# Dilated attention: row maxima subtracted and rows summed by VectorE, one exponential for three heads on ScalarE

## The reference, cut to what matters

```python
s = jnp.einsum('brhnqd,brhnkd->brhnqk', qb, kw).astype(F32) * (1.0 / math.sqrt(Dh))
s = jnp.where(mask, s, -1e30)
mx = jnp.max(s, axis=-1, keepdims=True)
p = jnp.exp(s - mx)
den = jnp.sum(p, axis=-1, keepdims=True)
o = jnp.einsum('brhnqk,brhnkd->brhnqd', (p / den).astype(v.dtype), vw)
lse = (mx + jnp.log(den))[..., 0]
...
alpha = jax.nn.softmax(jnp.stack(lses, axis=0), axis=0)
o_a = jnp.sum(alpha[..., None] * jnp.stack(outs, axis=0).astype(F32), axis=0).astype(dt)
```

## Time and profile before

| | us |
|---|---|
| median of three runs | 3615.83 |
| lowest, highest | 3612.37, 3620.40 |
| profiled execution | 3621.54 |
| its span, first to last instruction | 3619.9 |

### The profile page before, as it was taken

How to read it: one execution, slowest core, us unless ns; L and a number is a source line. 1 busy time by engine, 2 the same in 40 slices (tenths; PEclk the granted TensorE clock), 3 DMA queues, 4 the chain that set the end, 5 groups by cost and what they waited for, 6 DMA issues and landing times. The chain is left out here.

```text
span 3619.9 us, 45917 instructions
## 1 busy us (share of the span) xinstructions
PE 3258.0 (90%) x17716; PEld 2952.0 (82%) x17716; DVE 1596.1 (44%) x3321; ACT 1164.2 (32%) x2456; POOL 483.8 (13%) x854
## 2 busy tenths in 40 slices
PE   6899988998876999999978899879988779999998
PEld 6789876887766799999878898768877668999997
DVE  5345256453345334434453442564434453344434
ACT  4334423554422221111143334235553222121111
POOL 0111311211233000000001114112112220000000
PEclk9899998999997999999988999999999979999999
DMA  3434433333455122112043344333335551222111
GB/s 128 132 98 132 129 126 98 112 91 99 145 141 162 47 70 70 54 50 70 30 131 96 104 132 126 125 101 105 94 100 156 131 169 35 66 70 70 54 50 64
DMA packets 273050, 358.60 MB, mean 99 GB/s; under 512 B 27128, under 2 KB 209592, under 8 KB 272856
## 3 DMA queue, kind: packets, MB, share of 16 engines
q1 hardware_dynamic: 214520, 182.59, 17.0%
q0 software_dynamic: 58336, 173.45, 15.5%
HBM read 261.27 MB, written 94.69 MB: 98 GB/s over the span
## 5 line engine op out<-in xcount | busy, mean ns | idle before, releaser
L1648 PE MATMUL ps<-wh,xh 128*128 128x384 f32 (+1 forms) x1536 | 579.3, 377 | 19.3 <-DVE wl L1259 6.6
L1649 PE MATMUL ps<-wl,xh 128*128 128x384 f32 (+1 forms) x1536 | 563.8, 367 | 0.0
L1650 PE MATMUL ps<-wh,xl 128*128 128x384 f32 (+1 forms) x1536 | 563.7, 367 | 0.0
L1259 DVE TENSOR_TENSOR wl<-wraw,wh 128x1024 fp32r<-128x1024 f32 (+2 forms) x210 | 232.3, 1111 | 429.0 <-ACT wh L1000 429.0
L1648 PE MATMUL ps<-xh,wh 128*128 128x384 f32 (+1 forms) x1056 | 374.0, 354 | 38.2 <-DVE ol L1345 14.9
L1718 PE MATMUL ps<-xh,wh 128*128 128x384 f32 x1408 | 361.1, 337 | 20.1 <-DVE arena L1635 15.3
L1649 PE MATMUL ps<-xl,wh 128*128 128x384 f32 (+1 forms) x1056 | 360.3, 341 | 0.0
L1650 PE MATMUL ps<-xh,wl 128*128 128x384 f32 (+1 forms) x1056 | 360.2, 341 | 0.0
L1718 PE MATMUL ps<-xl,wh 128*128 128x384 f32 x1408 | 359.0, 336 | 0.0
L1718 PE MATMUL ps<-xh,wl 128*128 128x384 f32 x1408 | 358.8, 335 | 0.0
L1648 PEld LDWEIGHTS ps<-wh,xh 128*128 128x128 f32 x1536 | 299.0, 195 | 55.1 <-DVE ol L1345 7.1
(11 more groups left out here) (211 smaller groups left out, 5315.8 us busy)
## 6 DMA issues: line engine op xcount, KB each, us to landing
wraw<-in_w_in SPq DMA_DIRECT2D x96, 512.0 KB, 4.1
wraw<-in_w_ffn_in SPq DMA_DIRECT2D x88, 512.0 KB, 4.0
wraw<-in_w_in SPq DMA_DIRECT2D x72, 384.0 KB, 3.4
wraw<-in_w_ffn_out SPq DMA_DIRECT2D x44, 512.0 KB, 3.4
qkv_a<-stage POOLq DMA_DIRECT2D x108, 192.0 KB, 2.2
gate_t<-stage POOLq DMA_DIRECT2D x96, 192.0 KB, 2.2
stage<-gate_t POOLq DMA_DIRECT2D x96, 192.0 KB, 2.8
mix_t<-stage POOLq DMA_DIRECT2D x64, 192.0 KB, 3.8
```

Source lines behind the costliest of these rows:

```text
L1259: dve.tensor_tensor(wl[:, half, j, 0:w], wraw[:, n % RAW, 0:w], wh[:, half, j, 0:w].bitcast(F32), ALU.subtract).then_inc(w_lo, 1)
L1648: pe.matmul(out, ah, bh, start=first, stop=False)
L1649: pe.matmul(out, ah, bl, start=False, stop=False)
L1650: return pe.matmul(out, al, bh, start=False, stop=last)
```

## The change

ACT's six exponentials of a unit, with bias and accumulated sum, become two over three heads each, without either. DVE's two small instructions that wrote the negated scaled maxima become two subtractions of the maxima from the masked scores, in place in `a_p`, over three heads each; each raises `a_mx` as its predecessor did. In `a_turn` DVE waits for `a_pr` and sums the rows of all six heads in one instruction, ahead of its wait for the turn and its copy. In `a_out` DVE waits for its own sum ahead of its copy. The step list is the same.

```diff
--- before.py
+++ after.py
@@ -1087,12 +1087,10 @@
                         elif kind == "a_score":
                             u = step[1]
                             nk = len(UNITS[u][3])
-                            for h in range(A_H):
-                                if h % (A_H // 2) == 0:
-                                    act.wait_ge(a_mx, 2 * u + 1 + h // (A_H // 2))
-                                pr = a_p[:, h * nk * P:(h + 1) * nk * P]
-                                ins = act.activation(pr, pr, ACT.Exp, bias=unit_s[:, h:h + 1], scale=HD ** -0.5,
-                                                     accum_out=a_o[:, u % 2, A_W + A_H + h:A_W + A_H + h + 1])
+                            for i in range(2):
+                                act.wait_ge(a_mx, 2 * u + 1 + i)
+                                pr = a_p[:, i * (A_H // 2) * nk * P:(i + 1) * (A_H // 2) * nk * P]
+                                ins = act.activation(pr, pr, ACT.Exp, scale=HD ** -0.5)
                             ins.then_inc(a_pr, 1)
                         elif kind == "a_turn":
                             u = step[1]
@@ -1366,22 +1364,32 @@
                             if u >= 2:
                                 dve.wait_ge(a_stored[u % 2], 16 * A_STORES[u - 2][u % 2])
                             mk = masks[:, mask_of(g, s, t), :]
+
+                            def below(i):
+
+                                hs = slice(i * A_H // 2, (i + 1) * A_H // 2)
+                                part = a_p[:, hs.start * nk * P:hs.stop * nk * P].rearrange("p (h n) -> p h n", n=nk * P)
+                                top = a_o[:, u % 2, A_W + hs.start:A_W + hs.stop]
+                                return dve.tensor_tensor(part, part, top.unsqueeze(2).to_broadcast([P, A_H // 2, nk * P]),
+                                                         ALU.subtract)
+
                             for h in range(A_H):
                                 if h == A_H // 2:
                                     chain.wait()
-                                    dve.tensor_scalar(unit_s[:, 0:h], a_o[:, u % 2, A_W:A_W + h], -HD ** -0.5, None,
-                                                      ALU.mult).then_inc(a_mx, 1)
+                                    below(0).then_inc(a_mx, 1)
                                 sl = slice(h * nk * P, (h + 1) * nk * P)
                                 chain(dve.tensor_tensor_reduce(
                                     a_p[:, sl].rearrange("p (k n) -> p k n", k=nk),
                                     score_bank(nk, h).rearrange("p (k n) -> p k n", k=nk), mk, 1.0, -3e38, ALU.add, ALU.max,
                                     a_o[:, u % 2, A_W + h:A_W + h + 1]))
                             chain.wait()
-                            dve.tensor_scalar(unit_s[:, A_H // 2:A_H], a_o[:, u % 2, A_W + A_H // 2:A_W + A_H],
-                                              -HD ** -0.5, None, ALU.mult).then_inc(a_mx, 1)
+                            below(1).then_inc(a_mx, 1)
                         elif kind == "a_turn":
                             u = step[1]
                             nk = len(UNITS[u][3])
+                            dve.wait_ge(a_pr, u + 1)
+                            chain(dve.tensor_reduce(a_o[:, u % 2, A_W + A_H:], a_p[:, 0:A_H * nk * P].rearrange(
+                                "p (h n) -> p h n", h=A_H), AX_X, ALU.add))
                             dve.wait_ge(a_ptr, u + 1)
                             at = turned(nk)
                             dve.tensor_copy(a_pt[:, 512 * nk:768 * nk], side[:, at + 512 * nk:at + 768 * nk]
@@ -1389,6 +1397,7 @@
                         elif kind == "a_out":
                             u = step[1]
                             dve.wait_ge(a_pv, u + 1)
+                            chain.wait()
                             dve.tensor_copy(a_o[:, u % 2, 0:A_W], side[:, unit_out(u):unit_out(u) + A_W]).then_inc(a_ov, 1)
                         elif kind == "a_merge":
                             t = step[1]
```

## The result

| | changed | before, same session |
|---|---|---|
| median | 3637.42 us (3635.88 to 3642.30, 6 runs) | 3619.94 us (3612.37 to 3625.65, 6 runs) |
| profiled execution, span | 3637.06, 3635.4 us | 3621.54, 3619.9 us |
| ratio of the medians | 1.0049, 95% interval 1.0037 to 1.0061 | |

The changed kernel is slower by 17.5 us, with an interval of 13 to 22. The forecast was 8.9 us more, 3625 us, with a range up to 3635: the direction is right, the size is not, and the time lies outside the range. A second session gave 3637.65 us against 3617.36 (ratio 1.0049, 1.0036 to 1.0063).

The account below looks back on a forecast made before the run. TensorE, busy 90% of the span, was taken to bound the kernel. Two-tile turns 7.2, one-tile units 0 and row sums 1.7 us summed to 8.9 over the median 3615.8: 3625 us, 0.25% slower, range 3617 to 3635.

Parts of the forecast that it names:

- direct terms: Dilated attention: delays worked out at two-tile turns, one-tile units and row sums, 7.2 + 0 + 1.7 = 8.9 us.
- Two-tile turns: Turn of the probabilities in units with two key tiles: 3.92 us against 3.32, 0.60 later, 12 times, 7.2 us.
- One-tile units that wait: Units with one key tile: the fold, 0.79 us later, eats the turn's gain of 0.3; 0 us, bounds -1 to +1.
- The reduction behind which the copy waits: Row-sum reduction ahead of the copy in DVE's queue: PE's values product could start 6.83 us after a two-tile turn.
- rival on a fast subtraction: Subtraction at two elements a cycle, 0.55 us at 768 wide: not slower, 3610 us; chance 0.05.
- the part on the row sums: One reduction replaces accumulator reads and delays the copy; hidden where PE's clock is slow, 1.7 us in all.
- Six of the twelve two-tile intervals have the slow clock: From turn to values product, PE needs 7.13 us in six intervals, hiding the reduction; the others take 5.54 to 5.56.
- The arithmetic of the base: Profiled 3621.5 us would become 3630.4; less 5.7 us, its excess over the median 3615.8, the forecast is 3624.7.
- that of the clock: Rival: the clock falls more often behind longer idling at two-tile turns, 7.7 us more, 3632 us; chance 0.18.
- if the count of slow intervals leaves six by more than two: Sign in the profile after that the forecast is wrong: slow two-tile intervals differing from six by more than two.
- Half of it taken up: Rival: two-tile price 0.45 us, reduction hidden, one-tile units win 0.1 each: +4 to +5, 3620 us; chance 0.19.

Follow-up runs that it names:

- idle_dose: Kernel before, plus one ScalarE copy 600 wide behind the exponentials of each two-tile unit, delaying the turn by about 0.6 us: 3629.85 us, ratio 1.0028.
- late_sum: The changed kernel with the reduction behind the copy of the turned probabilities instead of ahead of it: 3628.02 us, ratio 1.0024 to before.
- no_sum: The changed kernel without VectorE's reduction, ones stored in place of the row sums: 3631.08 us, ratio 1.0035 to before.
- only_sum: Kernel before, its six exponentials keeping their bias but not the accumulator, with VectorE's reduction ahead of the copy: 3614.83 us, ratio 0.9989.
- sum_only_late: only_sum with the reduction behind the copy instead of ahead of it: 3598.42 us, ratio 0.9951 to before.
- filled kernels: Idle PE transposes ahead of two-tile turn waits in late_sum, before, the change and sum_only_late (there also ahead of one fold): 3624.31, 3615.25, 3642.84, 3605.46 us.
- groups_231: sum_only_late with the maxima handed over after heads 2, 5 and 6 instead of 3 and 6: 3602.75 us, ratio 0.9957 to before.
- idle_dose2: idle_dose with six more ScalarE copies 24 wide in each two-tile unit, the turn 1.26 us later than before: 3645.95 us, ratio 1.0080.

## Why the prediction was wrong

**The direct terms were right.** Two-tile turns: +0.60 us forecast, 0.59 to 0.63 in the units of the first trace. One-tile units that wait: the fold 0.76 to 0.82 us later (0.5 to 0.6 in unit 9), the turn back within 0.05 us of its old distance, 0 forecast and 0 seen. The reduction behind which the copy waits: 6.83 us from turn to product forecast, 6.77 seen. All edits together: the fixed part of the change is 7.6 us over before in the mean of three traces (7.0, 9.3, 6.5), against 8.9 forecast (the difference is less than what these three traces differ by). Single precision subtraction takes 959 ns for 768 elements. The Trainium skill (VectorE: DVE Perf Modes, section "The perf-mode tier table") has such a two-tensor operation at the single rate, and the row agrees. In the rival on a fast subtraction the price at 768 wide was set a little low: from L1558's own 492 ns at 512, with half of 1.04 ns for each further element, it would be about 0.62 us, an estimate, and not 0.55; nothing hung on it.

**The step that failed** is in the part on the row sums and in the sum: "Six of the twelve two-tile intervals have the slow clock", read from one trace, was taken as the kernel's habit and as unchanged by the change. Both halves were wrong. Of before, the five traces have 6, 1, 6, 3 and 2 slow intervals behind the long waits; mine was one of the two slowest. The change has 7, 6 and 8, and in its first two traces the one and the two long waits left are product waits, each of them with slow clock behind the product: none of its 24 long waits goes without. From 3.6 to 7.0 is 3.4 intervals at 1.57 us, 5.3 us. With the other slow time in the stages the traces give 34.0 us before and 47.3 after, and half of the difference is 6.7 us. Fixed part and slow time are 7.6 + 6.7 = 14.3 us; the stages' means say 712.4 - 698.2 = 14.2. The interval of the timed runs is 13 to 22, so some 3 us between 14.2 and 17.5 stay unassigned; the rest of the span does not show them. The traced executions themselves differ by only 14.0 us (3634.2 in the mean of three against 3620.3 in the mean of five), so those 3 us lie in which executions were traced.

By the terms of the sum, in the times: the turns were put at 7.2 us, and the three kernels with the turns alone (idle_dose, late_sum, no_sum) came at 10.1, 8.7 and 12.7. The row sums were put at 1.7 us, and cost 5 to 9 where they stand. The product waits at two-tile units in the change's traces are only 1.1 us in the mean of three; what the term cost beyond them is slow clock or scatter. How the clock's share divides between the turns and the reduction isn't settled: the three kernels with the turns alone have 38.0 us of slow time in their stages, one trace each, just 4 more than before. Behind the turns it is 21 us against 12 in before, elsewhere in the stages 17 against 22.

**The arithmetic of the base** hid this. I subtracted 5.7 us because the profiled execution lay that much over the median, as if that offset would carry over. The stages of that execution had 9.4 us more slow time than the mean of the five, 4.7 us of its length, and the changed kernel has that slow time anyway (43.9 to 50.7 us in its three traces, against 43.4): its profiled run lies 0.4 us below its own median. Besides, three runs put before at 3615.8 us, while the later sessions had 3617.2 to 3619.9.

**The rival that came closest** is that of the clock, but at other places. It expected units 3 and 4 to fall as well, 6.3 of its 7.7 us; with 1.26 us of idling they never did. It had the two remaining long waits at 0.3 and 1.1 us, because the trace it started from showed six slow ones already. Its chance of 0.18 was too low for a cost seen to depend on idling that the change lengthens. The test that I had named, "if the count of slow intervals leaves six by more than two", would not have caught it: the change's counts are within two of six, it is before's that is not.

**Half of it taken up** and **the fast subtraction** did not happen. In one-tile units 6 and 8 the product waits 0.42 and 0.38 us for the copy, and the next fold takes that up, as forecast.

## What to carry to other kernels

Before a cost is called hidden under a slow stretch, look whether the stretch is slow in every execution: two or three traces of the same kernel would have shown here that a cover worth 1.57 us was there in under half of the cases. A wait on TensorE's path costs its length and, where it is one of the longest, a chance of a spell at half clock behind it; shortening it gives both back. When an accumulator is moved off ScalarE, put the sum behind what the next engine waits for: the same two instructions in the other order are worth 14 us here (only_sum at -4.0 us, sum_only_late at -17.7).

## What the runs showed of the hardware

**The clock falls behind some waits and not behind others of the same length, and more often the longer PE has idled.** Counted over the turns of two-tile units, without the filled kernels, and without units 0, 1 and 5 of only_sum, where all six products wait. The three product waits of the change are counted as not slow:

| PE idle ahead of the turn, us | slow interval behind it | kernels |
|---|---|---|
| 0.67 | 0 of 20 | before, five traces |
| 1.26 | 0 of 24 | change (three), no_sum, late_sum, idle_dose |
| 1.58 to 1.63 | 0 of 10 | sum_only_late, groups_231 |
| 1.88 to 1.94 | 3 of 6 | groups_231, idle_dose2 |
| 2.11 | 17 of 30 | before |
| 2.45 to 2.50 (unit 2) | 1 of 6 | sum_only_late, groups_231, only_sum |
| 2.97 (unit 2) | 1 of 10 | before |
| 2.70 to 2.76 | 29 of 36 | as 1.26 |
| 3.57 (unit 2) | 11 of 12 | as 1.26 |
| 3.37, 4.24 | 8 of 8 | idle_dose2 |

Length alone doesn't decide: unit 2 at 2.97 us fell once in ten times, the others at 2.11 in 17 of 30. What PE and its clock had done ahead differs between them, and which part of that counts is open. The Trainium skill (TensorE: Matmul & The Clock Gate, section "What's actually happening") says that the throttled state is the default and that activity releases it; the counts agree in direction.

**One program, different clocks.** With identical instructions and identical idling, before had 23 to 44 us of slow clock in the two stages, 10 us of time. Its times over the sessions scatter by 18 us (3609.7 to 3627.3).

**The accumulator of an exponential is not free.** Its read shows as 187 ns each, and without it the exponentials of unit 0 follow each other every 0.41 us instead of every 0.49 at 256 wide; with the last read gone, too, the turn came 0.53 us earlier. The duration of the exponential's own row does not show it (498 ns without, 496 with).
